# The final factor of a decoder trunk: narrower sums, a written-out root and three tiles for GpSimd

## The reference

```python
h = rmsnorm(x, norm_mix)
parts = split(h @ w_in)                 # u, b_gate, c_gate, q/k/v of 3 head groups, gate_a, gate_b
branch_a = (b_gate * causal_dwconv(c_gate * u)) @ w_conv_out
branch_b = windowed_attention(q, k, v) @ w_attn_out
x = x + (sigmoid(gate_a) * branch_a + sigmoid(gate_b) * branch_b) @ w_out
up, gate = split(rmsnorm(x, norm_ffn) @ w_ffn_in)
x = x + (silu(causal_dwconv(gate) + b) * up) @ w_ffn_down
y = rmsnorm(x, norm_final)              # x * 1/sqrt(mean(x*x) + 1e-6) * norm_final, per token
```

## Time and profile before

| what | value |
|---|---|
| median of three runs | 1517.92 us |
| the profiled execution's own time | 1518.31 us |
| its span, first to last instruction | 1516.7 us |
| TensorE products busy | 99% of the span |
| VectorE / ScalarE / GpSimd busy | 59% / 49% / 5% |
| chain that ended last, TensorE's share | 96% |
| mean granted TensorE clock | 0.997 |
| output `y`: six stores | 2.16 MB |

### The profile page before, as it was taken

The page is one execution under the profiler, slowest core; times in us unless marked ns, Lnnn a source line. Parts: engine busy times, 40 slices in busy tenths (PEclk is TensorE's granted clock), DMA queues, the critical chain, the costliest instruction groups (busy, mean ns, idle before and its releaser), DMA issues.

```text
span 1516.7 us, 31579 instructions
## 1 busy us (share of the span) xinstructions
PE 1502.1 (99%) x12458; PEld 1499.5 (99%) x12458; DVE 893.1 (59%) x1058; ACT 750.3 (49%) x757; POOL 76.4 (5%) x144
## 2 busy tenths in 40 slices
PE   8999999999999999999999999999999999999997
PEld 8999999999999999999999999999999999999997
DVE  8646555656666545667666565664444666556564
ACT  7555554444555344455555454454444554445452
POOL 2000001001221000100000000000000000000000
PEclk9999999999999999999999999999999999999998
DMA  7867566557788855554677776775556666655552
GB/s 275 267 187 255 181 195 216 164 156 206 239 246 247 258 182 181 174 183 160 193 256 242 238 237 213 252 248 185 182 181 181 180 181 181 179 183 191 182 180 99
DMA packets 145304, 308.57 MB, mean 203 GB/s; under 512 B 10128, under 2 KB 10384, under 8 KB 144672
## 3 DMA queue, kind: packets, MB, share of 16 engines
q1 hardware_dynamic: 139264, 268.73, 56.4%
q0 software_dynamic: 5920, 38.05, 7.5%
HBM read 301.32 MB, written 26.38 MB: 216 GB/s over the span
## 4 chain that ended last, share of the span: by engine, by line
PE 96%; DMA 1%; DVE 1%; ACT 1%; issue 0%; SPq 0%; DVEq 0%; ACTq 0%
PE acc L998 31%; PE acc L996 31%; PE acc L997 31%; DMA raw<-w_ffn_in 1%; DVE w_split L600 1%; PE side L1072 0%; PE side L1091 0%; ACT w_split L379 0%; DMA raw<-w_in 0%; DVE yg L973 0%; PE side L1143 0%; PE side L1083 0%; PE side L1059 0%; PE side L1197 0%; PE side L1208 0%
## 5 line engine op out<-in xcount | busy, mean ns | idle before, releaser
L379 ACT ACTIVATE w_split<-raw 128x1024 fp32r<-128x1024 f32 x503 | 595.0, 1190 | 663.9 <-PE acc L998 622.7
L600 DVE TENSOR_TENSOR w_split<-raw,w_split 128x1024 fp32r<-128x1024 f32 x503 | 616.3, 1234 | 516.7 <-ACT w_split L379 510.7
L998 PE MATMUL acc<-h_rows,w_split 128*128 128x264 f32 x2872 | 820.0, 286 | 0.0
L996 PE MATMUL acc<-h_rows,w_split 128*128 128x264 f32 x2872 | 816.1, 284 | 2.8 <-DVE w_split L600 1.8
L997 PE MATMUL acc<-h_rows,w_split 128*128 128x264 f32 x2872 | 817.1, 284 | 0.0
L996 PEld LDWEIGHTS acc<-h_rows,w_split 128*128 128x128 f32 x2872 | 554.5, 193 | 4.2 <-issue 3.1
L998 PEld LDWEIGHTS acc<-h_rows,w_split 128*128 128x128 f32 x2872 | 557.2, 194 | 0.0
L997 PEld LDWEIGHTS acc<-h_rows,w_split 128*128 128x128 f32 x2872 | 555.8, 194 | 0.0
L998 PE MATMUL acc<-f_rows,w_split 128*128 128x264 f32 x704 | 201.0, 286 | 0.0
L997 PE MATMUL acc<-f_rows,w_split 128*128 128x264 f32 x704 | 200.3, 284 | 0.0
L996 PE MATMUL acc<-f_rows,w_split 128*128 128x264 f32 x704 | 199.2, 283 | 0.0
(11 more groups left out here) (195 smaller groups left out, 868.9 us busy)
## 6 DMA issues: line engine op xcount, KB each, us to landing
raw<-w_in SPq DMA_DIRECT2D x183, 512.0 KB, 3.9
raw<-w_ffn_in SPq DMA_DIRECT2D x176, 512.0 KB, 4.2
raw<-w_ffn_down SPq DMA_DIRECT2D x88, 512.0 KB, 3.7
raw<-w_out SPq DMA_DIRECT2D x32, 512.0 KB, 3.9
s_kv<-cache POOLq DMA_DIRECT2D x16, 1020.0 KB, 9.1
raw<-w_conv_out SPq DMA_DIRECT2D x16, 512.0 KB, 5.6
raw<-w_attn_out SPq DMA_DIRECT2D x8, 512.0 KB, 3.8
s_kv<-cache POOLq DMA_DIRECT2D x8, 508.0 KB, 5.7
```

Of the source, the lines that this page charges most:

```text
L379: act.activation(w_hi[:, s % RING], raw[:, s % RING], ACT.Copy).then_inc(hi_ready, 1)
L600: dve.tensor_tensor(w_lo[:, s % RING], raw[:, s % RING], w_hi[:, s % RING].bitcast(F32), ALU.subtract).then_inc(lo_ready, 1)
L996: pe.matmul(out, w_hi[:, slot, k, cols], backwards(m_hi[:, kt + k, :]), start=first and k == 0, stop=False)
L998: mm = pe.matmul(out, w_lo[:, slot, k, cols], backwards(m_hi[:, kt + k, :]), start=False, stop=last and k == 1)
```

## The change

`TOKENS` now gives start and number: the third column has the 8 sample tokens alone. In `token_sums` the middle two blocks load 8 stationary columns for it; the first and the last block still load 128, reading on into the next tile of `part` or `fsq`. For that the first tile of the last group goes to row 1 of `fsq`, the second to 2, the third to 3 and the fourth to 0 (`FSQ_ROW`). The root on ScalarE is written 128 times over, into `r_wide` [128, 3, 128], which lies where the rotary table was; the spreading loads that. The spreading is done twice, into two banks of PSUM. VectorE works from the first, on tiles 3 to 15 in pieces of 1, 2, 3, 4 and 3. ScalarE copies the second to `r` in SBUF, and GpSimd multiplies with that tiles 0, 1 and 2, each by itself. Three of ScalarE's last four rows come ahead of the root. SP sends eight stores in a fixed order (`STORES`).

```diff
-OUT_PIECES = ((0, 1), (1, 3), (3, 6), (6, 10), (10, 14), (14, 16))
-TOKENS = ((0, 0), (P, 0), (T - P, 2 * P - (T - P)))
+DVE_PIECES = ((3, 4), (4, 6), (6, 9), (9, 13), (13, 16))
+POOL_PIECES = ((0, 1), (1, 2), (2, 3))
+STORES = (("dve", 0), ("dve", 1), ("pool", 0), ("pool", 1), ("dve", 2), ("pool", 2), ("dve", 3), ("dve", 4))
+TOKENS = ((0, P), (P, P), (SEQ, BATCH))
+FSQ_ROW = (1, 2, 3, 0)
...
+        r_wide = place("r_wide", [P, len(TOKENS), P], at=rot_at)
...
-        STATS = 3 * 512
+        STATS, STATS_2 = 3 * 512, 512
...
-            for n, (q0, q1) in enumerate(OUT_PIECES):
-                sp.wait_ge(y_ready, n + 1)
+            for by, n in STORES:
+                ready, (q0, q1) = (y_ready, DVE_PIECES[n]) if by == "dve" else (y_pool_ready, POOL_PIECES[n])
+                sp.wait_ge(ready, n + 1)
                 sp.dma_start(y_out[:, q0:q1, :], yg[:, q0:q1, :]).then_inc(y_stored, 16)
...
-            def scale_rows(j):
-                for m in range(TILES):
-                    act.activation(yg[:, 4 * j + m, :], x[:, 4 * j + m, :], ACT.Copy,
-                                   scale=par_col(PAR_GF + 4 * j + m)).then_inc(yg_ready, 1)
+            def scale_rows(first, n):
+                for q in range(first, first + n):
+                    act.activation(yg[:, q, :], x[:, q, :], ACT.Copy, scale=par_col(PAR_GF + q)).then_inc(yg_ready, 1)
...
-                    sq_m = act.activation(fsq[:, m, :], x[:, 4 * j + m, :], ACT.Square)
+                    sq_m = act.activation(fsq[:, FSQ_ROW[m], :], x[:, 4 * j + m, :], ACT.Square)
...
-                if j < 3:
-                    scale_rows(j)
+                scale_rows(4 * j, TILES if j < 3 else 3)
             act.wait_ge(r2_ready, 3)
-            act.activation(r_tok[:, :], r_tok[:, :], ACT.Sqrt).then_inc(r_ready, 1)
-            scale_rows(3)
+            act.activation(r_wide[:, :, :], r_tok[:, :].unsqueeze(2).to_broadcast([P, len(TOKENS), P]), ACT.Sqrt).then_inc(r_ready, 1)
+            scale_rows(KT - 1, 1)
+            act.wait_ge(r_spread, 2)
+            act.activation(r[:, :], side[:, STATS_2:STATS_2 + T], ACT.Copy).then_inc(factor_ready, 1)
...
-            for q0, q1 in OUT_PIECES:
+            for q0, q1 in DVE_PIECES:
...
-            def token_sums(squares, first=False, last=False):
-                for c, (t0, _) in enumerate(TOKENS):
-                    mm = pe.matmul(side[:, 512 * c:512 * c + 1], squares[:, t0:t0 + P], ones[:, 0:1], start=first, stop=last)
+            def token_sums(flat, row, first=False, last=False):
+                for c, (t0, n) in enumerate(TOKENS):
+                    rows = P if first or last else n
+                    mm = pe.matmul(side[0:rows, 512 * c:512 * c + 1], flat[:, row * T + t0:row * T + t0 + rows], ones[:, 0:1],
+                                   start=first, stop=last)
...
-            for c, (t0, skip) in enumerate(TOKENS):
-                mm = pe.matmul(side[:, STATS + t0 + skip:STATS + t0 + P], r_tok[:, c:c + 1].to_broadcast([P, P]), ident[:, skip:P],
-                               start=True, stop=True)
-            mm.then_inc(r_spread, 1)
+            for at in (STATS, STATS_2):
+                for c, (t0, n) in enumerate(TOKENS):
+                    mm = pe.matmul(side[:, at + t0:at + t0 + n], r_wide[:, c, :], ident[:, 0:n], start=True, stop=True)
+                mm.then_inc(r_spread, 1)
...
+            pool.wait_ge(factor_ready, 1)
+            for q0, q1 in POOL_PIECES:
+                pool.wait_ge(yg_ready, q1)
+                pool.tensor_tensor(yg[:, q0, :], yg[:, q0, :], r[:, :], ALU.mult).then_inc(y_pool_ready, 1)
```

More of the change, by code:

```diff
@@ L276, in trunk_program @@
             sem("f_hi_ready"), sem("f_ready"))
-        yg_ready, y_ready = sem("yg_ready"), sem("y_ready")
+        yg_ready, y_ready, y_pool_ready, factor_ready = sem("yg_ready"), sem("y_ready"), sem("y_pool_ready"), sem("factor_ready")
         kv_stored, cache_copied, state_stored, y_stored = sem("kv_stored"), sem("cache_copied"), sem("state_stored"), sem("y_stored")
@@ L362, in _ @@
                     group(w_ffn_down, n, 2 * GW * i + GW, quad, s0=n, k0=TILES * first)
-            for n, (q0, q1) in enumerate(OUT_PIECES):
-                sp.wait_ge(y_ready, n + 1)
+            for by, n in STORES:
+                ready, (q0, q1) = (y_ready, DVE_PIECES[n]) if by == "dve" else (y_pool_ready, POOL_PIECES[n])
+                sp.wait_ge(ready, n + 1)
                 sp.dma_start(y_out[:, q0:q1, :], yg[:, q0:q1, :]).then_inc(y_stored, 16)
-            sp.wait_ge(y_stored, 16 * len(OUT_PIECES))
+            sp.wait_ge(y_stored, 16 * len(STORES))
             sp.wait_ge(kv_stored, 16 * NG)
@@ L885, in take @@
                         dve.wait_ge(part_ready, 11)
-                        dve.tensor_tensor(part[:, 0, :], part[:, 0, :], fsq[:, 0, :], ALU.add).then_inc(part_ready, 1)
+                        dve.tensor_tensor(part[:, 0, :], part[:, 0, :], fsq[:, FSQ_ROW[0], :], ALU.add).then_inc(part_ready, 1)
                     wait_tile(dve, group, quad, n, m)
@@ L1191, in _ @@
                 down("b", i, N_DOWN_B, PAIRS_A)
-            def token_sums(squares, first=False, last=False):
-                for c, (t0, _) in enumerate(TOKENS):
-                    mm = pe.matmul(side[:, 512 * c:512 * c + 1], squares[:, t0:t0 + P], ones[:, 0:1], start=first, stop=last)
+            def token_sums(flat, row, first=False, last=False):
[3 more added lines that the diff above has]
+                                   start=first, stop=last)
                 return mm
             pe.wait_ge(part_ready, 12)
-            token_sums(part[:, 0, :], first=True)
+            token_sums(part[:, :, :].rearrange("p a t -> p (a t)"), 0, first=True)
             for m in range(1, TILES):
                 pe.wait_ge(last_squared, m + 1)
-                mm = token_sums(fsq[:, m, :], last=m == TILES - 1)
+                mm = token_sums(fsq[:, :, :].rearrange("p a t -> p (a t)"), FSQ_ROW[m], last=m == TILES - 1)
             mm.then_inc(sumsq_ready, 1)
             pe.wait_ge(r_ready, 3)
-            for c, (t0, skip) in enumerate(TOKENS):
-                mm = pe.matmul(side[:, STATS + t0 + skip:STATS + t0 + P], r_tok[:, c:c + 1].to_broadcast([P, P]), ident[:, skip:P],
-                               start=True, stop=True)
-            mm.then_inc(r_spread, 1)
+            for at in (STATS, STATS_2):
+                for c, (t0, n) in enumerate(TOKENS):
+                    mm = pe.matmul(side[:, at + t0:at + t0 + n], r_wide[:, c, :], ident[:, 0:n], start=True, stop=True)
+                mm.then_inc(r_spread, 1)
         @block.gpsimd
```

## The result

The changed kernel takes 1521.48 us (median of 15 runs, 1521.12 to 1522.32), the kernel before 1517.61 (15 runs). The ratio is 1.0026, 95% interval 1.0019 to 1.0032: slower by 3.9 us. I had forecast 1519.0 and no difference beyond 0.2%, with 0.05 on slower by more. The span of the profiled execution went from 1516.7 to 1520.8.

A forecast was written before the change was run, and what follows sets the result against it. Tail bound by how early stores become available and the bytes behind them. Sums 0, root +0.33, first spreading 0, stores +0.80 gave +1.1 us: 1519.0 from a median of 1517.92, range 1517.0 to 1520.9.

The forecast's parts named there:

- What bounds the kernel: Kernel's tail: the end is set by how early stores become available and the bytes behind them; last landing before at 1516.4.
- D: Start of VectorE's first multiply in the tail, 1508.48 in the kernel before; forecast to move by +0.33 us.
- Sums: TensorE's sums by token, four records narrowed to 8 stationary columns: gain 0, ends 0.43 us gained and 0.4 lost.
- Root: ScalarE's root in the tail, written out wide: 0.53 us instead of 0.20, +0.33 on the path.
- What writing it out buys TensorE: Loads of the first spreading: the repeated column costs nothing now, so writing the root out gains 0; spreading stays 1.46 us.
- Scaling rows: Three ScalarE rows moved ahead of the root, 1.3 us, hidden in 2.09 us of idle time: cost 0.
- Second spreading and copy: TensorE's repeat spreading, then ScalarE's copy from PSUM, done at D + 1.68; GpSimd can start at D + 1.72.
- GpSimd: Its three multiplies in the tail: 0.75 us a tile, ends 0.62 and 1.33, done at D + 3.97; VectorE not slowed.
- The rival that did make GpSimd decide: GpSimd's tail multiplies held up: at 1.33 us a tile +2.3, 1520.2; chance 0.12 up to 1.7 a tile, 0.02 beyond.
- VectorE and stores: Tail: VectorE done at D + 3.99 against D + 4.88, but last landing at D + 8.72 against D + 7.92, +0.80 us.
- The hole: Sign in the tail's DMA stream: it runs dry near D + 2.6 to D + 3 while SP waits for GpSimd's tiles.
- The clock stays up: Rival: TensorE keeps 2.4 GHz through the tail's spreadings, -1.2 us, giving 1517.8; chance 0.12.

The follow-up runs named there:

- early drain: Changed kernel plus a drain of GpSimd right behind its last DMA, where it is hidden: 1518.2 us, ratio 1.0006 to the kernel before.
- clear and early drain: Kernel before plus a late one-column clear by GpSimd behind VectorE's fourth piece and a GpSimd drain behind its last DMA: 1517.13 us, ratio 0.9998.
- the other order: Changed kernel with its eight stores issued in the order in which their tiles become ready: 1521.14 us, ratio 1.0023 to the kernel before.
- the ten executions: Profiled executions of the kernel before, the changed one and eight experiments; the first spreading took 1.46 or 1.47 us in six, 0.85 to 0.96 in four.
- both repairs: Changed kernel with a GpSimd drain behind its last DMA and the eight stores in order of readiness: 1518.22 us, ratio 1.0006 to the kernel before.

## Why the prediction was wrong

**What bounds the kernel, and the sum as a whole.** The step that failed is in the first part: "the end is set by how early stores become available and by the bytes behind them". That held for the kernel before, and I carried it over to a kernel in which another engine stops late. (The sentence above that SP's wait for all stores ends the program holds for the kernel before alone, too: the program ends when all engines have met.) The sum has no term for what the program does after an engine's last instruction. For GpSimd it was 7.84 us, of which 2.8 stood out behind the last landing, where the sum had nothing. Its row was in the trace of before, under the closing line, which I had not read; in a stretch around the tail alone, a drain issued at 1365.7 doesn't appear. With it: last multiply D + 3.97, plus 7.84, plus 0.2 for the meeting of the engines is D + 12.0 = 1520.8 with D moved by 0.33, the measured span to 0.1 us, and as a median 1520.8 + 1.6 - 0.4 = 1522.0: inside the measured runs, 0.5 above their median.

**Sums.** Net 0 was right, for a reason that I had held open from both sides. TensorE's loads in the changed kernel, from the last full one before a narrow pair to the next full one:

```profile
1504.38 0.30 PEld L1204 LDWEIGHTS side<-ones,fsq 128*128 128x128 f32 x3
...
1504.71 0.19 PEld L1204 LDWEIGHTS side<-ones,fsq 128*128 128x128 f32 x1
```

The narrow pair between them, in the same view:

```profile
1504.59 0.10 PEld L1204 LDWEIGHTS side<-ones,fsq 128*8 128x8 f32 x2
```

The narrow pair starts at 1504.59, 0.21 behind the full-width load at 1504.38 (neighbours are 0.11 apart); both are done 0.10 later and the next full one starts at 1504.71. The two take 0.33 from full load to full load, as three intervals of 0.11 would. So narrow loads are cheaper, and the change of width gives it back. The Trainium skill ("TensorE: Matmul & The Clock Gate", LDWEIGHTS) has loading time go with the number of stationary columns; the trace agrees in the direction alone, with about 0.09 us for a load of 8 columns and 0.19 for one of 128. The Trainium skill ("TensorEngine Tiling (Array Packing)", Key Properties) says that a change of tiling mode drains TensorE; the 0.21 in front of the narrow pair would fit that, but no run shows that going from 128 columns to 8 is such a change. Of the chain's 24 records, 2.59 became 2.63; that is the last record, which ran after the clock had fallen. In four other executions with these sums the 18 records of `fsq` took 2.13, against 2.15 before.

**Root.** 0.53 foretold, 0.53 measured. **What writing it out buys TensorE:** nothing, as foretold; the loads are at 0.333 and the six records at 1.46 as before, and 0.85 with the written-out root (early drain) or without it (clear and early drain) when the clock is up.

**Scaling rows** were hidden. **Second spreading and copy:** D + 1.76 against D + 1.72. **GpSimd:** 0.74 a tile against 0.75, and VectorE's pieces kept 0.43, 0.70, 0.97 and 1.25 beside it, so nothing was held up. The rival that did make GpSimd decide was about its multiplies, at the wrong place: it priced the tiles and not what follows them.

**VectorE and stores.** Done at D + 3.99 as foretold, and worth nothing. The hole is there and the last landing released SP at D + 8.84 against 8.72. This step was right but cost nothing: it lay wholly under the drain, as the other order showed. With the drain repaired it is in the traces again (SP released 8.2 us behind D with the early drain alone, 7.9 with the order of readiness too), but the times of these two runs, both at a ratio of 1.0006, don't tell them apart.

**The chances.** "The clock stays up" got 0.12; it was so in four of the ten executions, one of them with the tail of the kernel before. I had taken one profiled execution for a property of the kernel.

## What to carry to other kernels

Before giving an engine its first work near the end of a program, look at what that engine does after its last instruction, in the view of the closing line over the whole span, not only in the last stretch. GpSimd's closing drain cost 0.08 us here for each DMA that it had issued since its last drain; if it must work late, drain it once in a hidden place behind its last DMA. And taking load off an engine pays only if that engine, not the bytes behind it, ends last: with both repairs VectorE was done at D + 3.99 in place of 4.88, and the stores ended no earlier.

## What else the runs showed

A drain of GpSimd costs by the *count* of its DMAs although they have long landed (0.07 + 0.082 us each, 0 to 95), and it can be paid in advance. Two 8-column loads were done in 0.10 us together, but the change of width cost TensorE about what they saved. And TensorE's clock level in a tail of one-column products varied between executions with the same code in the tail: 0.6 us on a spreading of six records.
